# State space: half of the gate product computed ahead during the scan chain, and three of eight final multiplications on GpSimd

## The chip, the cores and the metric

The kernel runs on one core of one Trainium2 chip. The time is the device time of one execution in microseconds (us). PE is TensorE, DVE is VectorE, ACT is ScalarE, POOL is GpSimd, and SP is SyncE, which here only issues transfers.

## What is computed

The program is one layer of a decoder trunk over 2048 positions: norm, input projection, attention, spatial gating and state space, output projection, feed-forward, and a gated embedding. The change lies in the state space (all fp32, 256 channels, 16 groups of 16 with 64 complex states each):

```
y = Re(C x) + D u                         # x: scan over the positions
y = gelu(y)                               # [2048, 256]
y = y * sigmoid(y @ glu_w + glu_b)        # the gate product, K = 256
```

## The kernel before

`state_space` (L1220) is one stage of its own; a barrier ends it. Positions are held as 256 chunks of 8 (`L`), the 256 chunks as two halves of 128 (`HM`), so that the output tile `Y` is [128, 2, 8, 256]. The 16 groups are worked off in 8 pairs (`Q`), called group 0 to 7 below.

DVE (L1511 to L1526) does two pairs at a time: it turns, scans along the chunks, and turns back into `entry`; a memset of `mark` (L1526) tells PE that two pairs are ready. PE (L1384 to L1399) then makes for each pair and chunk half a product with the entry states, two with the Toeplitz kernels and one more with the entry states (L1394, L1396, L1398) into bank q. ACT (L1440 to L1446) takes each bank through the gelu into `Y`.

The gate product needs `Y` with channels on the partitions. `turn_y(k)` (L1360) transposes channel half k in 16 tiles into banks 4k to 4k+3, and ACT copies these into `yT` (L1439 and L1449), which lies over the input `U`. Half 0 is turned ahead of pair 6 (`q == Q - 2`), half 1 behind pair 7. Also ahead of pair 6 stands `gate_product()` (L1376, work for the next stage's row tile 0, in bank 4), which DVE finishes in `finish_gate` and follows with `combine`. When all eight copies are there, PE runs the gate product (L1405 to L1410): 16 tiles of 128 positions, two channel halves each, two tiles to a bank:

```python
for n in range(HM * L):
    for k in range(2):
        mm = pe.matmul(bank[n // 2][...], yT[:, k, n * P:(n + 1) * P], glu_w[:, k, :], start=(k == 0), stop=(k == 1))
```

For each bank DVE adds the bias, which is spread over the partitions (`add_glu_bias`, L1529), ACT takes the sigmoid (L1453), and DVE multiplies `Y` by it (`apply_gate`, L1535), two banks behind the addition (L1540 to L1544). SP stores `Y` in four pieces (L1289 to L1292), each when its four positions of the chunk are done, and then loads row tile 0 for the next stage (L1294), `mix_and_project`, whose first ACT operation (L1718) waits for it.

POOL in this stage clears tiles, copies weights, adds the diagonal, masks four tiles (L1314) and does three steps of the normalisation of row tile 0 (L1318 to L1322); it has nothing after that. All queues are written out by hand; there is no planner. `Ba` and `Ca` of `StateParameters` (L702) are read by PE's first transposes and kernel products and by POOL's weight copies, and are idle later. The matmuls that the prediction compares with are those of L1345 (spreading of u, 64 output partitions) and L1182 (a lookup in the projection stage, over 33 partitions); the operations on POOL and DVE that it compares with are of the feed-forward (L2918, L2931, L2955; L2632, L2651) and of the projection (L1209).

Of the kernel before, what the change touches and what calls it, by code (L numbers as in the profile page):

```python
# [22 lines left out]
P = 128  # L23
# [647 lines left out]
CH = 16  # L671
# [26 lines left out]
class StateParameters:  # L698
# [4 lines left out]
    def __init__(self, nc, keep, p, ident, M):  # L703
        self.nc, self.p, self.ident = nc, p, ident
        self.Q, self.M = p["a_re"].shape[0] // 2, M
        Q, at = self.Q, SSM_AT
        self.turn_table = keep.over("turn", [P, 2, Q, M], F32, at)
        self.Ba = keep.over("Ba", [P, 2, Q, L, CH], F32, at + 2 * Q * M * 4)
        self.Ca = keep.over("Ca", [P, 2, Q, L + 1, CH], F32, at + 2 * Q * (M + L * CH) * 4)
        self.radius = keep.over("radius", [P, Q], F32, at + 2 * Q * (M + (2 * L + 1) * CH) * 4)  # L710
        assert at + (2 * Q * (M + (2 * L + 1) * CH) + Q) * 4 == SBUF_END
# [508 lines left out]
def state_space(nc, U, u_loaded, p, parameters, mix, ident, loads_ahead, part_stored, part_stores, mix_ahead, mix_ahead_loads):  # L1220
# [17 lines left out]
    MASK_AT, MASK_BANK, GATE_BANK = 2, Q - 1, 4  # L1238
    with Stage(nc, "ssm") as st:
# [22 lines left out]
            st.sem(n) for n in ("y_turned", "yT_copied", "entry_ready", "y_ready", "gelu_ready", "glu_done", "sig_ready", "out_ready"))  # L1262
        b_turned, b_copied, k_done, k_copied, share_done, share_copied = (
# [8 lines left out]
        @block.sync  # L1272
        def _(sp):
            z0, z0_src, z0_loaded = mix_ahead_loads[0]
            sp.dma_start(z0, z0_src).then_inc(z0_loaded, DMA)
            sp.dma_start(d_cols[:, :], p["d"].rearrange("(g c) -> c g", c=CH), allow_slow_non_contiguous=True).then_inc(d_loaded, DMA)
            sp.dma_start(glu_w[:, :, :], p["glu_w"].rearrange("(k p) n -> p k n", p=P)).then_inc(glu_loaded, DMA)
            sp.dma_start(glu_b[:, :], p["glu_b"].unsqueeze(0).to_broadcast([P, W])).then_inc(glu_loaded, DMA)
            for stored_part, count in zip(part_stored, part_stores):
                sp.wait_ge(stored_part, count)  # L1280
            for tile, src, loaded in mix_ahead_loads[1:]:
                sp.dma_start(tile, src, allow_slow_non_contiguous=True).then_inc(loaded, DMA)
            sp.wait_ge(kernel_ready, 1)
            sp.wait_ge(cleared, 1)
            for j in range(L):
                sp.dma_start(toeplitz[j * CH:(j + 1) * CH, :, j * CH:], kernel_rows[:, :, 0:(L - j) * CH]).then_inc(toeplitz_copied, DMA)
            for part, src, loaded in loads_ahead:
                sp.dma_start(part, src).then_inc(loaded, DMA)
            for h in range(HM):  # L1289
                for l in range(0, L, 4):  # L1290
                    sp.wait_ge(out_ready, h * L + l + 4)
                    sp.dma_start(mix_view[:, h, l:l + 4], Y[:, h, l:l + 4]).then_inc(stored[h], DMA)  # L1292
            sp.wait_ge(stored[0], L // 4 * DMA)
            sp.dma_start(ahead.row0[:, heads * HEAD + GW:], mix[0:P, :]).then_inc(ahead.row0_loaded, DMA)  # L1294

        @block.gpsimd
        def _(pool):
# [13 lines left out]
            pool.wait_ge(weights_ready, 4)  # L1311
            pool.wait_ge(mix_ahead.setup, 5 * DMA)
# [9 lines left out]
            nc.gpsimd.tensor_tensor(ahead.normed0[:, :, :], d, ahead.ln_shift.rearrange("p (g c) -> p g c", g=GROUPS), ALU.add).then_inc(ahead.normed_ready, 1)  # L1322

        @block.tensor
        def _(pe):
# [57 lines left out]

            for q in range(Q):  # L1384
                if q == MASK_AT:
                    turn_masks()
                if q == Q - 2:
                    turn_y(0)
                    gate_product()
                pe.wait_ge(entry_ready, q // 2 + 1)  # L1390
# [12 lines left out]
            pe.wait_ge(glu_loaded, 2 * DMA)  # L1403
            pe.wait_ge(yT_copied, 8)
            for n in range(HM * L):  # L1405
                for k in range(2):
                    mm = pe.matmul(bank[n // 2][:, (n % 2) * W:(n % 2 + 1) * W], yT[:, k, n * P:(n + 1) * P], glu_w[:, k, :],
                                   start=(k == 0), stop=(k == 1))
                if n % 2:
                    mm.then_inc(glu_done, 1)  # L1410

        @block.scalar
        def _(act):
# [17 lines left out]
            nc.scalar.activation(ahead.weight[:, :, :], ahead.drop[:, :, :], ACT.Exp, scale=-1.0).then_inc(ahead.weight_ready, 1)  # L1431
            for q in range(Q):
# [3 lines left out]
                if q == Q - 2:  # L1436
                    for n in range(4):
                        act.wait_ge(y_turned, n + 1)
                        nc.scalar.copy(yT.rearrange("p k t -> p (k t)")[:, n * BANK:(n + 1) * BANK], bank[n][:, :]).then_inc(yT_copied, 1)  # L1439
                act.wait_ge(y_ready, q + 1)  # L1440
# [15 lines left out]
        def _(dve):  # L1456
# [72 lines left out]
            def add_glu_bias(n):  # L1529
                h, l = divmod(2 * n, L)  # L1530
                dve.wait_ge(glu_done, n + 1)
                V.tensor_tensor(gate[:, h, l:l + 2, :], bank[n].rearrange("p (l w) -> p l w", l=2),
                                glu_b[:, :].unsqueeze(1).to_broadcast([P, 2, W]), ALU.add).then_inc(sig_ready, 1)

            def apply_gate(n):  # L1535
                h, l = divmod(2 * n, L)
                dve.wait_ge(rooted, 1 + n)
                V.tensor_tensor(Y[:, h, l:l + 2, :], Y[:, h, l:l + 2, :], gate[:, h, l:l + 2, :], ALU.mult).then_inc(out_ready, 2)

            for n in range(HM * L // 2 + 2):  # L1540
                if n < HM * L // 2:
                    add_glu_bias(n)
                if n >= 2:
# [1802 lines left out]
```

## Time and profile before

| | us |
|---|---|
| median of 3 runs | 2675.37 |
| lowest, highest | 2674.75, 2676.18 |
| the profiled execution's own time | 2676.85 |
| its span in the profile | 2675.3 |
| busy: PE, PE weight loads | 2532.1, 2169.0 |
| busy: DVE, ACT, POOL | 1794.4, 1352.9, 828.5 |

The profile is of one execution. The span runs from the first to the last recorded instruction; what lies around it is in the own time only. Busy times overlap between engines. An fp32 matmul leaves two records, a transpose one, so the gate product's 32 products are 64 records. In a list in order of time, instructions of one line that follow each other are merged; the second number is then the time that all of them took. The granted clock of PE is given as a share of 2.4 GHz.

### The profile page before, as it was taken

Reading aid. Unit: us, or ns where it says so; the run is one execution under the profiler, and the core shown is the slowest. Engines: PE = TensorE matmul, PEld = TensorE weight load, DVE = VectorE, ACT = ScalarE, POOL = GpSimd, SP = SyncE. Lnnn points to the kernel's source line nnn. Section 1 sums busy time; section 2 is a strip of 40 time slices with the busy share of each in tenths; the row PEclk is TensorE's granted clock in tenths of the full one; section 3 lists DMA queues with packets and bytes.
Section 4 is the critical chain, followed back from the end, with each engine's and each line's share of the span. In section 5 each row is a group of like instructions: output and inputs, shape, how many; then the busy total and the mean of one; then the engine's idle time right before and its main releaser. Section 6 shows DMA issues by size and latency. Waiting matters only on the chain. (4 is left out here: it accounts for less than half of the span.)

```text
span 2675.3 us, 38121 instructions
## 1 busy us (share of the span) xinstructions
PE 2532.1 (95%) x13395; PEld 2169.0 (81%) x13395; DVE 1794.4 (67%) x3337; ACT 1352.9 (51%) x2431; POOL 828.5 (31%) x625
## 2 busy tenths in 40 slices
PE   7999999999976899699999989999999999999998
PEld 6989979999965788488888868888888877887876
DVE  1113287777775776699999966879889975563333
ACT  4343424666645666455555546545555553444444
POOL 4454554655521111246555530002122210000000
PEclk9999999999987899799999999999999999999999
DMA  6675466788653454244444577543333336763221
GB/s 219 187 217 177 160 185 166 175 182 182 143 139 127 136 174 171 65 136 155 157 154 162 176 257 263 194 144 100 101 103 111 103 126 228 283 222 114 79 73 48
DMA packets 317450, 420.97 MB, mean 157 GB/s; under 512 B 31073, under 2 KB 229025, under 8 KB 312522
## 3 DMA queue, kind: packets, MB, share of 16 engines
q1 hardware_dynamic: 292090, 332.68, 41.4%
q0 software_dynamic: 25184, 86.01, 8.6%
q8 instruction: 102, 1.67, 0.3%
q14 instruction: 74, 0.61, 0.1%
HBM read 298.59 MB, written 124.16 MB: 158 GB/s over the span
## 5 line engine op out<-in xcount | busy, mean ns | idle before, releaser
L2834 PE MATMUL ffn_bank<-ffn_x,ffn_ring 128*128 128x512 f32 x704 | 278.1, 395 | 17.2 <-DVE ffn_strips L2632 8.9
L2836 PE MATMUL ffn_bank<-ffn_x,ffn_ring 128*128 128x512 f32 x704 | 277.2, 394 | 0.0
L2835 PE MATMUL ffn_bank<-ffn_x,ffn_ring 128*128 128x512 f32 x704 | 277.2, 394 | 0.0
L2908 POOL DMA_DIRECT2D ffn_act<-ffn_late x154 | 85.7, 558 | 476.1 <-DVE ffn_late L2664 445.4
L1203 POOL TENSOR_TENSOR in_w_lo<-in_w,in_w_hi 128x2048 fp32r<-128x2048 f32 x36 | 168.1, 4670 | 173.5 <-ACT in_w_hi L1071 173.5
L2834 PE MATMUL ffn_bank<-tail_shared,ffn_ring 128*128 128x512 f32 x528 | 206.3, 391 | 9.1 <-DVE ffn_ring L2607 7.5
L633 ACT ACTIVATE att_exps<-att_scores,att_part 128x256 f32<-128x256 f32 (+1 forms) x384 | 153.0, 454 | 105.1 <-DVE att_part L601 104.3
L2836 PE MATMUL ffn_bank<-tail_shared,ffn_ring 128*128 128x512 f32 x528 | 205.9, 390 | 0.0
L2431 ACT COPY ffn_strips<-ffn_bank 128x512 f32<-128x512 f32 x176 | 103.5, 588 | 147.6 <-PE ffn_bank L2836 147.6
L2648 DVE SCALAR_TENSOR_TENSOR ffn_strips<-ffn_strips,ffn_taps 128x512 f32<-128x512 f32 x176 | 144.6, 822 | 43.4 <-ACT ffn_strips L2446 43.4
L2834 PEld LDWEIGHTS ffn_bank<-ffn_x,ffn_ring 128*128 128x128 f32 x704 | 134.0, 190 | 49.0 <-issue 13.1
L2836 PEld LDWEIGHTS ffn_bank<-ffn_x,ffn_ring 128*128 128x128 f32 x704 | 134.1, 190 | 28.3
L2615 DVE TENSOR_TENSOR ffn_ring<-ffn_w,ffn_ring 128x2048 fp32r<-128x2048 f32 (+1 forms) x42 | 91.0, 2167 | 98.0 <-ACT ffn_ring L2405 98.0
L571 PE MATMUL att_bank<-att_v,att_expsT 128*128 128x66 f32 x1200 | 153.7, 270 | 2.8 <-issue 2.4
L2835 PEld LDWEIGHTS ffn_bank<-ffn_x,ffn_ring 128*128 128x128 f32 x704 | 134.0, 190 | 27.6
L571 PEld LDWEIGHTS att_bank<-att_v,att_expsT 128*128 128x128 f32 x1200 | 147.3, 192 | 4.5 <-issue 2.8
L1175 PE MATMUL in_bank<-in_w_hi,in_hi 128*128 128x256 f32 x512 | 145.8, 285 | 0.0
L2651 DVE SCALAR_TENSOR_TENSOR ffn_strips<-ffn_strips,ffn_taps 128x512 f32<-128x512 f32 x176 | 141.5, 804 | 6.2
L1176 PE MATMUL in_bank<-in_w_lo,in_hi 128*128 128x256 f32 x512 | 144.8, 283 | 0.0
L1177 PE MATMUL in_bank<-in_w_hi,in_lo 128*128 128x256 f32 x512 | 144.8, 283 | 0.0
L2396 ACT CAST ffn_ring<-ffn_sums 128x512 fp32r<-128x512 f32 x176 | 107.9, 614 | 62.5 <-PE ffn_bank L2836 52.0
L2835 PE MATMUL ffn_bank<-ffn_x_lo,ffn_ring 128*128 128x512 f32 x352 | 136.9, 389 | 0.0
(441 smaller groups left out, 7369.3 us busy)
## 6 DMA issues: line engine op xcount, KB each, us to landing
ffn_w<-in_ffn_w_up SPq DMA_DIRECT2D x88, 512.0 KB, 4.8
ffn_act<-ffn_late POOLq DMA_DIRECT2D x154, 256.0 KB, 2.3
in_w<-in_w_in SPq DMA_DIRECT2D x36, 1024.0 KB, 6.6
ffn_a_raw<-ffn_act SPq DMA_DIRECT2D x77, 256.0 KB, 3.5
ffn_a_raw_later<-ffn_act SPq DMA_DIRECT2D x77, 256.0 KB, 4.4
ffn_w<-ffn_down_sums SPq DMA_DIRECT2D x16, 1024.0 KB, 5.1
ffn_w<-in_ffn_w_down SPq DMA_DIRECT2D x12, 1024.0 KB, 5.8
ffn_pieces<-in_ffn_w_down POOLq DMA_DIRECT2D x44, 256.0 KB, 3.6
```

The costliest lines, as they stand in the source:

```text
L571: mm = pe.matmul(out, expsT[:, n % 2, piece * P:(piece + 1) * P], vals[:, b, blk, h * ROW:(h + 1) * ROW], start=(at == 0), stop=(at == len ...
L633: nc.scalar.activation(exps[:, n % RING, m * width:(m + 1) * width], scores[:, n % RING, m * width:(m + 1) * width], ACT.Exp, bias=part[:, ...
L1175: pe.matmul(out[:, 0:WIDE], x_hi[:, k, part], w_hi[w][:, k, :], start=(k == 0), stop=False)
L1176: pe.matmul(out[:, 0:WIDE], x_hi[:, k, part], w_lo[w][:, k, :], start=False, stop=False)
L1177: mm = pe.matmul(out[:, 0:WIDE], x_lo[:, k, part], w_hi[w][:, k, :], start=False, stop=(k == KC - 1))
L1203: nc.gpsimd.tensor_tensor(w_lo[B % 2][:, :, :], w_raw[B % 2][:, :, :], w_hi[B % 2][:, :, :].bitcast(F32), ALU.subtract).then_inc(w_lo_read ...
L2396: nc.scalar.copy(slot(j)[0], src).then_inc(w_hi_ready, 1)
L2648: nc.vector.scalar_tensor_tensor(conv[:, n, tg], raw[f % 2][:, n, 1 + tg * BANK:1 + (tg + 1) * BANK], tap[1], conv[:, n, tg], ALU.mult, AL ...
L2651: nc.vector.scalar_tensor_tensor(conv[:, n, tg], raw[f % 2][:, n, tg * BANK:(tg + 1) * BANK], tap[0], conv[:, n, tg], ALU.mult, ALU.add).t ...
L2834: pe.matmul(out[:, :], hi[:, k], x_hi[kind][:, k], start=(k == 0 and fresh), stop=False, skip_group_check=not fresh)
L2835: pe.matmul(out[:, :], hi[:, k], x_lo[kind][:, k], start=False, stop=False, skip_group_check=not fresh)
L2836: mm = pe.matmul(out[:, :], lo[:, k], x_hi[kind][:, k], start=False, stop=(k == KH - 1), skip_group_check=not fresh)
```

## The change

The first channel half of the gate product is computed during the scan chain. The turn of half 0 moves from pair 6 up to pair 4. There PE makes, for banks 0 to 3 (position tiles 0 to 7), a product of a row of ones with the bias (one partition, 256 columns) and on top of it that of channel half 0; ACT copies each bank to the new tile `glu_sums`. Ahead of pair 6, behind `gate_product()`, the same is done for tiles 8 to 15 in the same four banks. At the end PE makes only the products of channel half 1, and each group of four tiles waits for its own copy of `yT` (from the ninth tile on, for all). DVE adds the kept sum instead of the bias. `glu_sums` and the ones lie over `Ba` and `Ca`. POOL multiplies banks 1, 3 and 5 by their gates instead of DVE, and SP waits for both counts.

```diff
     def __init__(self, nc, keep, p, ident, M):        # StateParameters
+        glu_at, glu_end = at + 2 * Q * M * 4, at + 2 * Q * (M + (2 * L + 1) * CH) * 4
+        self.glu_first = keep.over("glu_first", [P, M * L // P, 2 * P], F32, glu_at)
+        self.ones = keep.over("glu_ones", [P, P], F32, glu_at + M * L * 2 * 4)
...
+    EARLY_AT, LATE_AT, EARLY_BANKS = Q // 2, Q - 2, 4
+    POOL_GATES = (1, 3, 5)
...
                 for l in range(0, L, 4):
-                    sp.wait_ge(out_ready, h * L + l + 4)
+                    s = (h * L + l) // 4
+                    sp.wait_ge(out_ready, 2 * s + 2 - sum(n < 2 * s + 2 for n in POOL_GATES))
+                    sp.wait_ge(pool_out_ready, sum(n < 2 * s + 2 for n in POOL_GATES))
...
             pool.wait_ge(weights_ready, 4)
+            nc.gpsimd.memset(ones[0:1, :], 1.0).then_inc(ones_ready, 1)
...
+            for n in POOL_GATES:
+                h, l = divmod(2 * n, L)
+                pool.wait_ge(rooted, n + 1)
+                nc.gpsimd.tensor_tensor(Y[:, h, l:l + 2, :], Y[:, h, l:l + 2, :], gate[:, h, l:l + 2, :], ALU.mult).then_inc(pool_out_ready, 1)
...
+            def first_glu_products(first):
+                for b in range(first, first + EARLY_BANKS):
+                    for i in range(2):
+                        n = 2 * b + i
+                        out = bank[b % EARLY_BANKS][:, i * W:(i + 1) * W]
+                        pe.matmul(out, ones[0:1, :], glu_b[0:1, :], start=True, stop=False)
+                        mm = pe.matmul(out, yT[:, 0, n * P:(n + 1) * P], glu_w[:, 0, :], start=False, stop=True)
+                    mm.then_inc(early_done, 1)
+
             for q in range(Q):
...
-                if q == Q - 2:
+                if q == EARLY_AT:
                     turn_y(0)
+                    pe.wait_ge(glu_loaded, 2 * DMA)
+                    pe.wait_ge(ones_ready, 1)
+                    pe.wait_ge(yT_copied, 4)
+                    first_glu_products(0)
+                if q == LATE_AT:
                     gate_product()
+                    pe.wait_ge(early_kept, EARLY_BANKS)
+                    first_glu_products(EARLY_BANKS)
...
             turn_y(1)
-            pe.wait_ge(glu_loaded, 2 * DMA)
-            pe.wait_ge(yT_copied, 8)
+            pe.wait_ge(early_kept, 2 * EARLY_BANKS)
             for n in range(HM * L):
-                for k in range(2):
-                    mm = pe.matmul(bank[n // 2][:, (n % 2) * W:(n % 2 + 1) * W], yT[:, k, n * P:(n + 1) * P], glu_w[:, k, :],
-                                   start=(k == 0), stop=(k == 1))
+                if n % 4 == 0:
+                    pe.wait_ge(yT_copied, 4 + n // 4 + 1 if n < 2 * EARLY_BANKS else 8)
+                mm = pe.matmul(bank[n // 2][:, (n % 2) * W:(n % 2 + 1) * W], yT[:, 1, n * P:(n + 1) * P], glu_w[:, 1, :], start=True, stop=True)
...
+            def keep_first_glu(first):
+                for b in range(first, first + EARLY_BANKS):
+                    act.wait_ge(early_done, b + 1)
+                    nc.scalar.copy(glu_sums[:, 2 * b:2 * b + 2, :], bank[b % EARLY_BANKS].rearrange("p (l w) -> p l w", l=2)).then_inc(early_kept, 1)
...
-                if q == Q - 2:
+                if q == EARLY_AT:
                     for n in range(4):
                         act.wait_ge(y_turned, n + 1)
                         nc.scalar.copy(yT...)
+                    act.wait_ge(weights_ready, 4)
+                    keep_first_glu(0)
+                if q == LATE_AT:
+                    keep_first_glu(EARLY_BANKS)
...
             def add_glu_bias(n):
+                dve.wait_ge(early_kept, n + 1)
                 dve.wait_ge(glu_done, n + 1)
                 V.tensor_tensor(gate[:, h, l:l + 2, :], bank[n].rearrange("p (l w) -> p l w", l=2),
-                                glu_b[:, :].unsqueeze(1).to_broadcast([P, 2, W]), ALU.add).then_inc(sig_ready, 1)
+                                glu_sums[:, 2 * n:2 * n + 2, :], ALU.add).then_inc(sig_ready, 1)
...
-                if n >= 2:
+                if n >= 2 and n - 2 not in POOL_GATES:
                     apply_gate(n - 2)
```

## Rows read from the trace of the kernel before

**Rows 1.** The waits between 744 and 842 us: total us, times, longest.

```profile
DVE ssm_share L1532 <- PE ssm_bank L1407: 10.7, 8, 6.5
...
PE ssm_bank L1394 <- DVE ssm_mark L1526: 7.6, 2, 6.0
```

**Rows 2.** DVE in order of time: start, us, line, operation, [idle before <- releaser].

```profile
803.49 0.06 DVE L1526 MEMSET ssm_mark<- 128x1 f32 x1
...
827.03 0.69 DVE L1532 TENSOR_TENSOR ssm_share<-ssm_bank,ssm_glu_b 128x512 f32<-128x512 f32 x1 [0.44 <-PE ssm_bank L1407]
827.64 1.89 DVE L1538 TENSOR_TENSOR ssm_Y<-ssm_Y,ssm_share 128x512 f32<-128x512 f32 x3
```

**Rows 3.** PE in order of time, the same columns.

```profile
782.11 0.70 PE L1394 MATMUL ssm_bank<-ssm_Ca_pair,ssm_spun 128*128 128x256 f32 x2 [1.62 <-DVE ssm_mark L1526]
...
787.02 0.60 PE L1398 MATMUL ssm_bank<-ssm_Ca_pair,ssm_spun 128*128 128x256 f32 x2
793.57 1.22 PE L1394 MATMUL ssm_bank<-ssm_Ca_pair,ssm_spun 128*128 128x256 f32 x2 [5.96 <-DVE ssm_mark L1526]
...
800.77 1.91 PE L1365 MATMUL ssm_bank<-whole_ident,ssm_Y 128*128 128x128 f32 x16
802.51 1.00 PE L1381 MATMUL ssm_bank<-ixers_ahead_normed,mixers_ahead_maskT 128*128 128x64 f32 x8
803.61 0.70 PE L1394 MATMUL ssm_bank<-ssm_Ca_pair,ssm_spun 128*128 128x256 f32 x2
...
810.08 1.94 PE L1365 MATMUL ssm_bank<-whole_ident,ssm_Y 128*128 128x128 f32 x16 [0.97 <-ACT ssm_Y L1444]
812.94 14.05 PE L1407 MATMUL ssm_bank<-ssm_glu_w,whole_u 128*128 128x256 f32 x64 [0.93 <-ACT whole_u L1449]
```

**Rows 4.** ACT in order of time, the same columns.

```profile
787.65 0.79 ACT L1444 ACTIVATE ssm_Y<-ssm_bank 128x128 f32<-128x128 f32 x4 [1.83 <-PE ssm_bank L1398]
...
809.15 0.79 ACT L1444 ACTIVATE ssm_Y<-ssm_bank 128x128 f32<-128x128 f32 x4 [1.83 <-PE ssm_bank L1398]
810.75 2.06 ACT L1449 COPY whole_u<-ssm_bank 128x512 f32<-128x512 f32 x4 [0.81 <-PE ssm_bank L1365]
812.82 1.28 ACT L1453 ACT_TABLE_LOAD   x1
```

**Rows 5.** SP's issue of row tile 0 and ACT's wait for it.

```profile
829.93 0.46 SPq L1294 DMA_DIRECT2D mixers_ahead_row<-ssm_out  x1
...
835.04 0.63 ACT L1718 ACTIVATE mixed_squares<-mixers_ahead_row 128x512 f32<-128x512 f32 x1 [6.65 <-DMA mixers_ahead_row<-ssm_out]
```

**Rows 6.** Two other products: the spreading of u, and the lookup of the bias.

```profile
762.16 3.67 PE L1345 MATMUL ssm_bank<-whole_u,ssm_BaT 128*64 128x256 f32 x32 [0.23 <-ACT ssm_kernel_rows L1422]
...
L1182 PE MATMUL in_bank<-in_lookup,in_per_head x6: 804/844/844, 12.2 to 15.3; 33*8 33x384 f32 x6
```

**Rows 7.** POOL's and DVE's operations of 512 columns beside each other.

```profile
L2918 POOL TENSOR_TENSOR ffn_late<-ffn_late x22: 1286/1296/1847, 1153.4 to 2190.3; 128x512 f32<-128x512 f32 x22
...
L1209 POOL TENSOR_TENSOR in_result_lo<-in_result,in_result_hi x32: 1268/1300/2408, 41.2 to 402.0; 128x512 fp32r<-128x512 f32 x32
...
1479.07 1.07 POOL L2955 TENSOR_TENSOR ffn_pieces<-ffn_pieces 128x256 f32<-128x256 f32 x1
...
1487.43 1.56 POOL L2931 TENSOR_TENSOR ffn_late<-ffn_late 128x512 f32<-128x512 f32 x1
...
1479.46 0.68 DVE L2632 TENSOR_TENSOR ffn_strips<-ffn_bank,ffn_strips 128x512 f32<-128x512 f32 x1
...
1487.87 1.67 DVE L2651 SCALAR_TENSOR_TENSOR ffn_strips<-ffn_strips,ffn_taps 128x512 f32<-128x512 f32 x1
...
1490.84 0.75 DVE L2651 SCALAR_TENSOR_TENSOR ffn_strips<-ffn_strips,ffn_taps 128x512 f32<-128x512 f32 x1
```

**Rows 8.** Granted clock (PEclk) in short stretches, with each engine's busy time.

```profile
782.00:787.60 5.60, 5.49 (x32) 4.75 (x32) 5.53 (x7) 0.79 (x4) 4.14 (x3) 1.00 0.20 82
...
791.00:793.40 2.40, 0.00 (x0) 0.00 (x0) 2.36 (x3) 0.00 (x0) 0.00 (x0) 0.50 0.00 0
```

More of the change, by code:

```diff
@@ L710, in __init__ @@
         self.radius = keep.over("radius", [P, Q], F32, at + 2 * Q * (M + (2 * L + 1) * CH) * 4)
+        glu_at, glu_end = at + 2 * Q * M * 4, at + 2 * Q * (M + (2 * L + 1) * CH) * 4
+        self.glu_first = keep.over("glu_first", [P, M * L // P, 2 * P], F32, glu_at)
+        self.ones = keep.over("glu_ones", [P, P], F32, glu_at + M * L * 2 * 4)
+        assert glu_at + (M * L * 2 + P) * 4 <= glu_end
         assert at + (2 * Q * (M + (2 * L + 1) * CH) + Q) * 4 == SBUF_END
@@ L1262, in state_space @@
             st.sem(n) for n in ("y_turned", "yT_copied", "entry_ready", "y_ready", "gelu_ready", "glu_done", "sig_ready", "out_ready"))
+        glu_sums, ones = parameters.glu_first, parameters.ones
+        ones_ready, early_done, early_kept, pool_out_ready = (st.sem(n) for n in ("ones_ready", "early_done", "early_kept", "pool_out_ready"))
         b_turned, b_copied, k_done, k_copied, share_done, share_copied = (
@@ L1537, in apply_gate @@
                 dve.wait_ge(rooted, 1 + n)
-                V.tensor_tensor(Y[:, h, l:l + 2, :], Y[:, h, l:l + 2, :], gate[:, h, l:l + 2, :], ALU.mult).then_inc(out_ready, 2)
+                V.tensor_tensor(Y[:, h, l:l + 2, :], Y[:, h, l:l + 2, :], gate[:, h, l:l + 2, :], ALU.mult).then_inc(out_ready, 1)
             for n in range(HM * L // 2 + 2):
```

## The prediction, made before the changed kernel was run

> **What bounds the kernel now.** The change lies in one stage, the state space, some 80 us of a span of 2675.3. I read the waits of that stage first, then each engine's instructions in order of time. The waits [rows 1] show that the engines hand over to each other: in the middle PE waits 7.6 us for DVE's mark, which closes a pair of groups, and at the end DVE waits 10.7 us for the gate product, 6.5 of it for the first bank.
>
> So the stage has two parts. Up to 803.5 DVE sets the pace: it has no gaps between its scan chains, and the last mark stands at 803.49 [rows 2]. PE idles in that part: groups 2 and 3 end at 787.0 + 0.6 = 787.6, groups 4 and 5 start at 793.57 when their mark comes [rows 3]. After 803.5 it is PE. Groups 6 and 7, their gelu and the start of the second turn take 803.61 to 810.08, that is 6.47; the gate product starts at 812.94, 2.86 behind the turn, because it waits for all four of ACT's copies; its 64 records run to 827.0 [rows 3, 4]. DVE only follows: its last bias addition starts at 827.03, 0.04 behind PE, then sigmoid, and three multiplications, the last of which ends at 827.64 + 1.89 = 829.53 [rows 2]. SP then issues the load of row tile 0 (829.93), and the next stage opens on it: ACT's first square starts at 835.04, 5.1 behind the issue, after 6.65 of waiting [rows 5]. What is won or lost at 829.53 is therefore won or lost in the kernel.
>
> **The change, part by part.** The price of a matmul first. The fp32 product of 256 columns leaves two records; 64 records from 812.94 to 812.94 + 14.05 are 0.2195 each, 0.439 a product [rows 3].
> - *Gone from the end*: the first channel half, 16 products, 16 x 0.439 = 7.02 us.
> - *Added earlier*: the same 16 products, 7.02, and 16 products of the ones row with the bias, 256 columns each. I take 0.439 for these too, another 7.02. No row has a product over one partition. The lower end is the pair of 64-wide outputs over 256 columns, 32 records in 3.67, 0.115 each [rows 6]: half price, 3.7 us in all. The nearest by partitions is the lookup product over 33: five steps between 12.2 and 15.3, 0.62 for 384 columns, 1.61 ns a column against 0.86 in the gate product [rows 6]. That would be 13.2 us. It is nearly twice the gate product's pace, as the lower of the clock's two levels would make it, so I read it as clock and not as a price of few partitions; it does say that few partitions are not cheap.
>
> *Where the added work lies.* The turn of the first half moves from 800.77 up to group 4. It needs the gelu of group 3, which ends at 787.65 + 0.79 = 788.44 [rows 4]; with the 0.14 that lay between gelu and turn before (809.94 to 810.08) it starts at 788.58. Copies and first product follow 2.86 later, 791.44, as at the end of before. The first batch (8 bias, 8 halves) is 7.02: PE is free at 798.46. Groups 4 and 5 were ready at 793.46, and now wait 5 us for PE. They take 5.4, as groups 2 and 3 did (782.11 to 787.6 [rows 3]): 803.9. The gate statistics' product 1.1 (802.51 to 803.61): 805.0. The second batch 7.02: 812.0. Groups 6 and 7 with gelu 6.47: the second turn starts at 818.5, not at 810.08. PE's idle 6 us and the low-clock stretch in groups 4 and 5 are used up, and **PE becomes the bound from 788 to the end**; 8.4 us later is what the 14 us of early work cost beyond the cover.
>
> *What comes back.* The first product no longer waits for all copies, only for one of the second half: 16 transposes end 16 x 0.11 = 1.8 after the turn's start (1.91 for 16 before), the first copy is done by then (0.67 + 0.6). So 818.5 + 1.8 = 820.3, a gain of 1.1; the 16 remaining products end at 827.3. The last addition starts 0.04 after, about 827.4, against 827.03. The eight additions read a kept sum in place of the bias; partitions and columns are the same, so 0.69 each.
>
> *Copies of the kept sums*, 8 x 0.6 on ACT [rows 4]: four lie in ACT's idle time before group 4's gelu; PE waits for the first four before the second batch, but they end near 799. The second four end about 0.6 behind the batch, before group 6's gelu is due. ACT's table load for the sigmoid (1.28 behind the last copy) ends near 822.5; the first addition ends at 822.1, so the first sigmoid is 0.4 late, and catches up at 0.63 against 0.88 a bank. Nothing at the end. SP has one more wait, POOL one memset of one partition that only the masks follow, the four semaphores no row: no time.
>
> *The three multiplications on POOL.* DVE had 0.61 a multiplication (1.89 for three). PE now gives a bank every 0.88, not 1.75, and DVE's 16 operations at 0.61 to 0.65 would take 10 us for banks that come in 7: without the move the end would be near 831. With it DVE has 13. POOL's 512-column operation takes 1.29 alone [rows 7], but the two engines stop each other. With both operands in the state buffer, DVE's 0.75 became 1.67 from 1487.87, under POOL's operation from 1487.43 to 1488.99, whereas an addition with one operand in PSUM kept its 0.68 under POOL [rows 7]. So the additions go free, the multiplications take turns. In order: multiplication 0 on DVE until 824.4; POOL's 1 until 825.7; DVE's 2 until 826.3; POOL's 3 until 827.6; DVE's 4 until 828.2; the last addition behind it until 828.9, its sigmoid until 829.6; POOL's 5 until 829.5; DVE's 6 until 830.1 and 7 until 830.7. Against 829.53: **+1.2**. Bounds: nothing in each other's way gives 827.4 + 0.69 + 0.04 + 0.63 + 0.04 + 0.68 = 829.5, no loss; POOL at 2.4 each, the longest of its 32 operations of this size [rows 7], three in a row from 823.7, gives 830.9 and two multiplications, 832.1, +2.6.
>
> The Trainium skill (SBUF — State Buffer, "Who interferes with whom") calls this an exclusive lock between a GpSimd instruction that reads SBUF and a VectorE instruction with two SBUF inputs. By that rule the end is +1.2, without it +0; these rows agree with it.
>
> **The sum.** -7.0 (products) + 8.4 (second turn late) - 1.1 (first product earlier) = +0.3, tail +0.9 on top: +1.2. The profiled execution took 2676.85 (span 2675.3 and 1.55 around it), 1.48 above the median of 2675.37; the sum makes it 2678.05, and the median **2676.6**. Nothing behind the stage is changed, and its opening load follows the end of the multiplications as before. About 0.2% (5.35 us) is what a measurement of this kernel can tell from no change: faster begins below 2670.0, slower above 2680.7.
>
> **The rivals.**
> - *A, the forecast*: PE, not DVE, bounds the middle, and the gain at the end is paid for ahead of it. 0.72.
> - *B, the bias products cost little.* At half price the second turn comes 3.5 earlier: -2.3, 2673.1, still no change. At no price it would start at 811.4, bound by the mark at 803.49 + 0.1 and what follows: with a tail like A's 830.7 - 7.0 = 823.7, -5.8, 2669.6, faster. For: the spreading products (L1345) at half. Against: they write 64 partitions at a time, first one half of the bank's rows and then the other; here all 128 are written. 0.05 for half, 0.04 for none.
> - *C, slower: the clock.* In before PE's granted clock fell from 1.00 to 0.50 (2.4 to 1.2 GHz) after it had idled from 787.6; 791.0 to 793.4 is at 0.50 [rows 8]; group 4's first products, behind it, took 1.22 where those of group 2 took 0.70 [rows 3], which DVE hid. Now PE has only 16 short transposes in the 3.8 us between 787.6 and 791.44, and what runs then is on the path. Half of all time at 0.50 is lost: a spell of 6 us from 791 costs 3, giving 2679.6: no change still. It decides from (5.35 - 1.2) x 2 = 8.3 us at 0.50: the whole first batch, 14 us at that level, costs 7.0 and gives 2683.6. For: the row at 791.0; against: 782.0 to 787.6 was at 1.00 behind a pause of 1.6 [rows 3, 8]. 0.12 for the short spell, 0.04 for the long one.
> - *D, the early part does not get early* (a mark or a copy comes so late that the batches queue behind it): the marks do not depend on PE, so this only gives what A has. 0.03, up to 2681.5.
>
> The Trainium skill (TensorE: Matmul & The Clock Gate, "Part 4: PE-mode transpose") says that a transpose doesn't count as PE work for the clock as other matmuls do. By this rule C's short spell would happen and the time be 2679.6. No row before decides: the transposes at 800.77 ran at 1.00 behind other products.
>
> **How the numbers follow.** A with its bounds (-1.2 for no conflict on DVE, +1.4 for POOL at its slowest) reaches from 2675.4 to 2678.0; C's short spell lies at 2679.6 and B at half price at 2673.1. Range 2673.0 to 2680.3: it takes these in with 0.7 for the terms' errors on the upper side, and leaves out C long, B at no price and most of D. Faster: B at no price, and 0.01 for errors at A's lower end, 0.05. Slower: C long, and 0.02 for half of D and the 33-partition price, 0.06. Same: 0.89.
>
> **What would show it.** Right: matmul records of the batches from about 791.4 to 798.5 and 805 to 812 without a gap, bias ones at 0.22; group 4's products start near 798.5, 5 behind their mark; second turn near 818.5; 32 records of the final product in 7.0; POOL's multiplications near 1.3, and DVE's beside them over 1; last multiplication near 830.7. Wrong: a second turn before 815 (bias products cheap), granted clock at 0.50 between 791 and 812 (C), a last multiplication at 829.5 or 832 (tail mis-sized), or a difference that arises behind 835, which none of this covers.

## The result, and the profile after

The changed kernel takes 2697.54 us (median of 4, 2695.03 to 2700.12) against 2675.77 for the kernel before (median of 4, the three of the table above and one more): a ratio of 1.0081, interval 1.0067 to 1.0094. It is slower by some 21 us, where +1.2 and no measurable change were forecast. The profiled execution took 2698.17, with a span of 2696.6: 21.3 us more than the 2675.3 of before.

Where the 21.3 lie can be read from four points. The stage begins with PE's first transposes. In the profile of before:

```profile
748.93 3.03 PE L1330 MATMUL ssm_bank<-whole_ident,whole_Ba 128*128 128x128 f32 x16 [2.65 <-PEq L143]
```

PE of the changed kernel in order of time (start, us, line, operation and count, [idle before <- releaser]); it answers to [rows 3]:

```profile
751.85 3.47 PE L1345 MATMUL ssm_bank<-whole_ident,whole_Ba 128*128 128x128 f32 x16 [2.65 <-PEq L143]
...
791.08 1.97 PE L1380 MATMUL ssm_bank<-whole_ident,ssm_Y 128*128 128x128 f32 x16 [0.88 <-ACT ssm_Y L1483]
793.97 0.67 PE L1404 MATMUL ssm_bank<-ssm_glu_b,whole_glu_ones 1*128 1x256 f32 x2 [0.92 <-ACT whole_u L1474]
794.57 0.70 PE L1405 MATMUL ssm_bank<-ssm_glu_w,whole_u 128*128 128x256 f32 x2
...
796.45 1.22 PE L1404 MATMUL ssm_bank<-ssm_glu_b,whole_glu_ones 1*128 1x256 f32 x2
797.60 1.22 PE L1405 MATMUL ssm_bank<-ssm_glu_w,whole_u 128*128 128x256 f32 x2
...
810.11 1.06 PE L1425 MATMUL ssm_bank<-ssm_Ca_pair,ssm_spun 128*128 128x256 f32 x2
...
817.02 1.00 PE L1396 MATMUL ssm_bank<-ixers_ahead_normed,mixers_ahead_maskT 128*128 128x64 f32 x8
817.95 0.69 PE L1404 MATMUL ssm_bank<-ssm_glu_b,whole_glu_ones 1*128 1x256 f32 x2
...
824.62 1.22 PE L1404 MATMUL ssm_bank<-ssm_glu_b,whole_glu_ones 1*128 1x256 f32 x2
...
831.39 1.06 PE L1425 MATMUL ssm_bank<-ssm_Ca_pair,ssm_spun 128*128 128x256 f32 x2
...
839.03 1.94 PE L1380 MATMUL ssm_bank<-whole_ident,ssm_Y 128*128 128x128 f32 x16 [0.97 <-ACT ssm_Y L1483]
840.81 7.07 PE L1438 MATMUL ssm_bank<-ssm_glu_w,whole_u 128*128 128x256 f32 x32
```

DVE of the changed kernel, the same columns; it answers to [rows 2]:

```profile
806.08 0.06 DVE L1565 MEMSET ssm_mark<- 128x1 f32 x1
...
841.94 0.69 DVE L1572 TENSOR_TENSOR ssm_share<-ssm_bank,whole_glu_first 128x512 f32<-128x512 f32 x1 [18.97 <-PE ssm_bank L1438]
...
849.07 1.76 DVE L1578 TENSOR_TENSOR ssm_Y<-ssm_Y,ssm_share 128x512 f32<-128x512 f32 x2
```

and ACT's first square of the next stage, which answers to [rows 5]:

```profile
856.00 0.63 ACT L1758 ACTIVATE mixed_squares<-mixers_ahead_row 128x512 f32<-128x512 f32 x1 [6.18 <-DMA mixers_ahead_row<-ssm_out]
```

The stage starts 2.9 later (751.85 against 748.93), before any edited line runs. Its last multiplication ends at 849.07 + 1.76 = 850.83 against 829.53. So the stage, from first transpose to last multiplication, is 98.98 us against 80.60, **+18.4**. The first square follows 5.2 behind (5.5 before), and from there to the end it is 1840.6 against 1840.3. All that the change did is in the stage. The 2.9 ahead of it is scatter: in a second profile of the kernel before (before_again, below) the stage starts at 751.60.

Inside the stage the last mark stands 54.2 behind the first transpose, as before (54.6): DVE's chain is untouched. What is late is PE's second turn, at 839.03, 33.0 behind the last mark; before it was 6.6, and the forecast had 15.0 (818.5 - 803.49). From the second turn to the end it is 11.8 against 19.45; forecast 12.2. The gain at the end came as foreseen, 7.65. The price ahead of it was 26.4, not 8.4.

Read the batches in PE's rows. A pair of records of the bias product and a pair of the half alternate. From 793.97 they follow each other at 0.60 to 0.63 us a pair, from 796.45 at 1.15; the forecast had 0.439. PE's weight loads (PEld) show where the first part of that comes from, in the gate product of before and then in the changed kernel:

```profile
812.91 13.68 PEld L1407 LDWEIGHTS ssm_bank<-ssm_glu_w,whole_u 128*128 128x128 f32 x64 [1.13 <-issue]
```

```profile
794.57 0.30 PEld L1405 LDWEIGHTS ssm_bank<-ssm_glu_w,whole_u 128*128 128x128 f32 x2 [0.33 <-issue]
795.20 0.29 PEld L1404 LDWEIGHTS ssm_bank<-ssm_glu_b,whole_glu_ones 1*128 1x128 f32 x2 [0.33 <-issue]
```

In before the 64 loads, 0.19 each, keep the pace of the matmuls above them (13.68 us in all). In the changed kernel no load runs for 0.33 ahead of each pair, and a pair's loads start only when the pair before is nearly done (794.57, the time at which PE's row of that pair begins too).

For the second part, the clock says what the doubling from 0.6 to 1.15 is (stretch, length, busy us and instructions of PE, its loads, DVE, ACT, POOL, then the granted clock, DMA share and GB/s):

```profile
793.97:796.45 2.48, 2.48 (x8) 1.15 (x9) 2.40 (x5) 0.00 (x0) 0.00 (x0) 1.00 0.00 0
796.45:810.10 13.65, 13.65 (x25) 6.34 (x25) 9.42 (x14) 1.75 (x3) 0.00 (x0) 0.50 0.00 0
...
817.95:824.40 6.45, 6.45 (x21) 3.04 (x20) 4.67 (x9) 1.23 (x3) 0.00 (x0) 0.95 0.00 0
824.60:831.40 6.80, 6.80 (x14) 3.34 (x14) 0.00 (x0) 0.58 (x1) 0.00 (x0) 0.50 0.00 0
```

Two things came together. At a granted clock of 1.00 a pair takes 0.625 and not 0.439; and from 796.4 and again from 823.8 the clock is at 0.50 (1.2 in place of 2.4 GHz), although PE was busy all of that time (13.65 of 13.65 us in the first stretch).

### The profile page after: what moved, and what is told of

Its sections match the earlier page's. It is cut to its first block and busy times, and to the rows that moved or that the text cites. A ratio compares the mean times of both kernels' runs of the same rounds, so it can differ in the third digit from the quotient of the medians.

```text
span 2696.6 us, 38199 instructions
## 1 busy us (share of the span) xinstructions
PE 2551.5 (95%) x13427; PEld 2175.8 (81%) x13427; DVE 1793.8 (67%) x3334; ACT 1357.6 (50%) x2439; POOL 831.9 (31%) x629
## 3 DMA queue, kind: packets, MB, share of 16 engines
q8 instruction: 102, 1.67, 0.3%
## 5 line engine op out<-in xcount | busy, mean ns | idle before, releaser
L2875 PEld LDWEIGHTS ffn_bank<-ffn_x,ffn_ring 128*128 128x128 f32 x704 | 133.3, 189 | 27.3
```

Of the source, the lines that this page charges most:

```text
L2875: pe.matmul(out[:, :], hi[:, k], x_lo[kind][:, k], start=False, stop=False, skip_group_check=not fresh)
```

## The experiments

The stage's length is compared from the profiles, since it is free of the scatter before and behind. T is the second turn's distance from the last mark, E the distance from the second turn to the end of the last multiplication. Each ratio is to runs of the kernel before made beside that variant (their medians are 2675.8, 2675.9, 2676.4 and 2678.5), so it isn't the quotient of two medians of this column.

| kernel | first transpose | last multiplication's end | stage | T | E | median us | ratio to before (interval) |
|---|---|---|---|---|---|---|---|
| before | 748.93 | 829.53 | 80.60 | 6.6 | 19.45 | 2675.77 | |
| before_again | 751.60 | 831.87 | 80.27 | 6.6 | 19.4 | 2677.02 (one run) | |
| after | 751.85 | 850.83 | 98.98 | 33.0 | 11.8 | 2697.54 | 1.0081 (1.0067 to 1.0094) |
| after_again | 751.43 | 844.89 | 93.46 | 26.7 | 11.8 | 2689.82 (one run) | |
| no_bias | 754.39 | 829.46 | 75.07 | 9.0 | 11.8 | 2674.24 | 0.9985 (0.9970 to 1.0000) |
| rows128 | 751.54 | 833.53 | 81.99 | 16.0 | 11.8 | 2678.47 | 1.0003 (0.9987 to 1.0018) |
| rows64 | 751.81 | 838.16 | 86.35 | 20.3 | 11.8 | 2687.19 | 1.0036 (1.0022 to 1.0050) |
| rows32 | 751.42 | 845.79 | 94.37 | 28.3 | 11.8 | 2695.25 (one run) | |
| ones_first | 751.38 | 838.91 | 87.53 | 21.5 | 11.8 | 2684.98 | 1.0026 (1.0013 to 1.0039) |
| bias_dve | 750.77 | 824.50 | 73.73 | 7.4 | 11.8 | 2674.63 | 0.9992 (0.9983 to 1.0001) |
| bias_dve_again | 750.88 | 825.97 | 75.09 | 9.0 | 11.8 | 2674.32 | 0.9990 (0.9980 to 1.0000) |
| bias_dve_dve_gates | 753.39 | 828.15 | 74.76 | 7.4 | 13.1 | 2673.10 | 0.9992 (0.9983 to 1.0001) |
| pool_gates_only | 752.63 | 833.70 | 81.07 | 7.0 | 19.0 | 2679.57 | 1.0012 (1.0003 to 1.0021) |

One more thing varies between the profiles and has to be kept apart. In six of the thirteen, PE's clock is at 0.50 for some 3 us in groups 2 and 3, ahead of every batch, although all their products are over 128 partitions: before_again, no_bias, rows128, rows32, ones_first and bias_dve_again. The kernel before itself does it in one profile and not in the other:

```profile
786.00:788.00 2.00, 2.00 (x8) 1.72 (x8) 1.97 (x2) 0.00 (x0) 1.84 (x3) 0.50 0.01 4
```

(before_again, the same columns as above; the first profile has 1.00 there.) DVE hides it in before. In the changed program the first turn follows group 3, so there it costs 1.67 us: from the start of group 2 to the first turn it is 6.38 in after and 8.05 in rows128.

The theory (P): the bias product stands on one partition, between products over 128. The weights of a product of another height are not loaded ahead, and a PE on which one partition works in half of the products is given the lower clock. The rivals: any batch put early costs this (E), or the number of products does (W).

**no_bias**: the bias products taken out (and the bias with them).

```diff
-                        pe.matmul(out, ones[0:1, :], glu_b[0:1, :], start=True, stop=False)
-                        mm = pe.matmul(out, yT[:, 0, ...], glu_w[:, 0, :], start=False, stop=True)
+                        mm = pe.matmul(out, yT[:, 0, ...], glu_w[:, 0, :], start=True, stop=True)
```

> The changed kernel without the 16 bias products (the bias is left out of the result). Theory P (the product over one partition, between products over 128, makes each weight load wait for the matmul ahead of it, 0.3125 us a record in place of 0.2195, and PE so thinly filled falls to the lower clock): without them a batch of 8 halves takes 8 x 0.439 = 3.5 us, the granted clock stays 1.00 from 791 on, the second turn comes about 8 us behind the last mark as in before, and the time is 2670 or a little under. Rival E (any early batch ahead of a group does it: little work behind 16 transposes drops the clock, whatever the products are over): the halves run at 0.58 a record, the batches take 7 each, and the time is 2680 or more.

PE of this run, in order of time:

```profile
798.19 3.69 PE L1404 MATMUL ssm_bank<-ssm_glu_w,whole_u 128*128 128x256 f32 x16 [0.92 <-ACT whole_u L1473]
...
807.79 3.67 PE L1404 MATMUL ssm_bank<-ssm_glu_w,whole_u 128*128 128x256 f32 x16
...
817.67 1.94 PE L1380 MATMUL ssm_bank<-whole_ident,ssm_Y 128*128 128x128 f32 x16 [0.97 <-ACT ssm_Y L1482]
```

Each batch is 3.7, the pace of before, and the stage is 5.5 shorter than before. E falls: an early batch behind 16 transposes costs its products and no more. The whole was 2674.24, where 2670 was expected, 0.9985 of before, with an interval that ends at 1.0000: the stage shows the gain, the whole time barely. T is 9.0, where bias_dve below, with the same program on PE, has 7.4: this is the 1.67 of groups 2 and 3 at the lower clock.

**rows128**: the same product, spread over all partitions.

```diff
-            nc.gpsimd.memset(ones[0:1, :], 1.0)
+            nc.gpsimd.memset(ones[0:128, :], 1.0 / 128)
...
-                        pe.matmul(out, ones[0:1, :], glu_b[0:1, :], start=True, stop=False)
+                        pe.matmul(out, ones[0:128, :], glu_b[0:128, :], start=True, stop=False)
```

> The bias product over 128 partitions, each row of ones being 1/128: the same number of products and columns, the same result. Theory P: no change of height between products, batches of 7.0 us, clock 1.00, second turn at about 12 us behind the last mark, time 2676 to 2678, what the prediction said. Rival W (it is the number of products and the accumulation on a just started bank that cost, not the one partition): batches of 13 to 16 us as in the changed kernel, time 2697.

```profile
795.85 0.59 PE L1405 MATMUL ssm_bank<-ssm_glu_w,whole_u 128*128 128x256 f32 x2
796.28 0.59 PE L1404 MATMUL ssm_bank<-ssm_glu_b,whole_glu_ones 128*128 128x256 f32 x2
...
801.89 0.59 PE L1405 MATMUL ssm_bank<-ssm_glu_w,whole_u 128*128 128x256 f32 x2
...
821.73 1.94 PE L1380 MATMUL ssm_bank<-whole_ident,ssm_Y 128*128 128x128 f32 x16 [0.97 <-ACT ssm_Y L1483]
```

A pair each 0.43, the batch 7.0, as the prediction priced it; the stage 82.0, **+1.4 where the prediction said +1.2**, the ratio 1.0003. That the two agree so closely is luck: 1.67 of rows128's stage is the lower clock in groups 2 and 3. Without it the stage would be near 80.3 and T 14.3, so the forecast sum was about 1.5 too high (T 0.7, the tail 0.4, the marks 0.3). The 12 for T in the expectation of this run was too low. The number of products, the weight loads and the accumulation are those of the changed kernel; only the partitions differ. W falls, and the 17 us between 99.0 and 82.0 (11.5 with the second profile of the changed kernel) hang on the height of sixteen products.

**ones_first**: in each batch the eight bias products first, then the eight halves.

```diff
...
+                for n, out in tiles:
+                    pe.matmul(out, ones[0:1, :], glu_b[0:1, :], start=(n % 2 == 0), stop=False, skip_group_check=True)
+                for n, out in tiles:
+                    mm = pe.matmul(out, yT[:, 0, ...], glu_w[:, 0, :], start=False, stop=(n % 2 == 1), skip_group_check=True)
...
```

> The eight bias products of a batch in a row, then its eight halves: the same instructions, two changes of height a batch in place of sixteen. If the slow pace comes from each change of height (P1), records are at 0.22 again and a batch takes 7.0 to 7.5 us at full clock; the clock then says whether one-partition products count less for it: if not, time 2677; if they do, it falls during or behind the eight, and the time lies at 2680 to 2690. If the slow pace belongs to every one-partition product wherever it stands (P2), the eight take 0.31 a record or more, and the halves 0.22.

PE in order of time, and then stretches with the granted clock:

```profile
795.19 3.69 PE L1402 MATMUL ssm_bank<-ssm_glu_b,whole_glu_ones 1*128 1x256 f32 x16 [0.92 <-ACT whole_u L1474]
798.80 5.41 PE L1404 MATMUL ssm_bank<-ssm_glu_w,whole_u 128*128 128x256 f32 x16
804.05 0.59 PE L1425 MATMUL ssm_bank<-ssm_Ca_pair,ssm_spun 128*128 128x256 f32 x2
...
810.22 4.96 PE L1402 MATMUL ssm_bank<-ssm_glu_b,whole_glu_ones 1*128 1x256 f32 x16
```

```profile
795.19:798.90 3.71, 3.71 (x17) 2.95 (x17) 3.63 (x6) 0.00 (x0) 0.00 (x0) 1.00 0.00 0
799.00:802.00 3.00, 3.00 (x8) 2.38 (x9) 2.86 (x7) 0.59 (x1) 0.00 (x0) 0.50 0.00 0
...
814.00:818.00 4.00, 4.00 (x10) 2.71 (x10) 1.20 (x2) 0.59 (x1) 0.00 (x0) 0.50 0.00 0
```

Sixteen one-partition records run in 3.69, 0.22 each: a product over one partition is no dearer and no cheaper than one over 128, and in the first batch no slow pace is left. That is P1: the slow pace belongs to the change of height. But the clock still falls: in the first batch it is 1.00 in the eight bias products and 0.50 from 799 on, while halves over 128 partitions run; in the second it falls already within the eight, which take 4.96. The slow pace is gone and the fall is not, so the fall isn't caused by exposed loads. The time, 2685, is at the middle of the third outcome expected.

**rows64** and **rows32**: as rows128, with 64 partitions and 1/64, or 32 and 1/32.

> The bias product over 64 partitions with 1/64. If only products over the whole height let the next weight load go ahead (P1 with any smaller height), the pace stays 0.31 and the clock decides the rest: if it follows the pace, 2697; if it follows the number of rows at work, which is now near three quarters, it stays at 1.00 and the time is 2682 to 2684 (6 us of exposed loads over the forecast). If the pace is 0.22, the price is of one partition alone.

PE over 64 partitions, and the clock in both batches:

```profile
793.95 0.67 PE L1404 MATMUL ssm_bank<-ssm_glu_b,whole_glu_ones 64*128 64x256 f32 x2 [0.92 <-ACT whole_u L1474]
794.55 0.70 PE L1405 MATMUL ssm_bank<-ssm_glu_w,whole_u 128*128 128x256 f32 x2
795.18 0.70 PE L1404 MATMUL ssm_bank<-ssm_glu_b,whole_glu_ones 64*128 64x256 f32 x2
...
803.87 0.59 PE L1425 MATMUL ssm_bank<-ssm_Ca_pair,ssm_spun 128*128 128x256 f32 x2
```

```profile
793.95:803.87 9.92, 9.92 (x32) 4.92 (x33) 9.67 (x15) 1.75 (x3) 0.00 (x0) 1.00 0.00 0
810.04:819.99 9.95, 9.95 (x34) 4.93 (x33) 4.67 (x9) 1.81 (x4) 0.00 (x0) 1.00 0.00 0
```

In this profile the two terms come apart. The pairs follow each other at 0.628 as over one partition, and the clock stays at 1.00 in both batches and beside them. So a product of half height costs the same exposed load as one of one partition, and here it cost no clock. The batch, 9.9, is 2.9 above rows128's 7.0, for 16 changes of height: 0.18 each, about as long as one weight load of the gate product in before (0.190 on average). So what is paid at each change is about one weight load that is no longer hidden. The two batches make 6.0 us; the stage is only 4.4 above that of rows128 because rows128 had the 1.67 in groups 2 and 3. The whole time missed the expected 2682 to 2684: the median of ten runs is 2687.19 (2682.30 to 2691.09), and the profiled one, 2682.91, is the second fastest. Whether the clock fell in the slower ones isn't known, since only one was profiled.

> The bias product over 32 partitions with 1/32. The pace stays at 0.31 as over 64 and over 1 (height changes). If the clock follows the share of rows at work, it lies between one partition (falls) and 64 (stays at 1.00): with 32 of 128 in half of the products it may go either way; stays: stage 86 to 88 us; falls: 95 to 99.

```profile
795.24:805.00 9.76, 9.76 (x32) 4.76 (x33) 9.51 (x15) 1.76 (x3) 0.00 (x0) 1.00 0.00 0
816.50:826.00 9.50, 9.50 (x18) 4.54 (x18) 0.00 (x0) 1.17 (x2) 0.00 (x0) 0.50 0.00 0
```

The stage is 94.4, in the range expected if the clock falls. With 32 partitions the clock held in the first batch and was at 0.50 in the second: between the two, as far as two batches can tell.

**bias_dve**: no bias products; DVE adds the bias to the kept sums in the time in which it waits for PE.

```diff
...
             combine()
+            dve.wait_ge(glu_loaded, 2 * DMA)
+            for n in range(HM * L // 2):
+                dve.wait_ge(early_kept, n + 1)
+                kept = glu_sums[:, 2 * n:2 * n + 2, :]
+                V.tensor_tensor(kept, kept, glu_b[:, :].unsqueeze(1).to_broadcast([P, 2, W]), ALU.add).then_inc(bias_added, 1)
...
-                dve.wait_ge(early_kept, n + 1)
+                dve.wait_ge(bias_added, n + 1)
```

> The changed kernel without bias products; DVE adds the bias to the eight kept sums behind its work for row tile 0, where it waited 19 us before the last bank-by-bank additions. Theory: 8 additions at 0.61 to 0.69 fit between about 5 us behind the last mark and the end of the second turn (9 behind the mark in the run without bias), so the stage is as long as in that run, 75.1 us from the first transpose to the last multiplication against 80.6 before: 5.5 us less, 2670.4. Rival: the additions end behind the first bank of the final product and delay the tail by up to 2 us: 77, 2672.

DVE in order of time, and PE's second turn:

```profile
805.32 0.06 DVE L1562 MEMSET ssm_mark<- 128x1 f32 x1
...
810.20 4.90 DVE L1569 TENSOR_TENSOR whole_glu_first<-whole_glu_first,ssm_glu_b 128x512 f32<-128x512 f32 x8
815.60 0.69 DVE L1575 TENSOR_TENSOR ssm_share<-ssm_bank,whole_glu_first 128x512 f32<-128x512 f32 x1 [0.51 <-PE ssm_bank L1435]
...
822.74 1.76 DVE L1581 TENSOR_TENSOR ssm_Y<-ssm_Y,ssm_share 128x512 f32<-128x512 f32 x2
```

```profile
812.69 1.94 PE L1379 MATMUL ssm_bank<-whole_ident,ssm_Y 128*128 128x128 f32 x16 [0.97 <-ACT ssm_Y L1480]
```

The eight additions end at 815.10 and the first of the final ones starts at 815.60, still waiting for PE: they cost nothing. The stage is 73.7, **6.9 shorter than before and 20 to 25 shorter than the changed kernel**, at the full result. The 75.1 expected was no_bias's, with the lower clock in groups 2 and 3; this profile doesn't have it. T is 7.4 against 6.6, so PE is nearly back on DVE's mark.

In the whole this is worth less than it should be: the median is 2674.63 and not 2670.4, the ratio 0.9992. Repeated:

> The version with the bias on DVE again, since its first ratio (0.9992, interval 0.9983 to 1.0001) is smaller than its stage's gain (6.9 of 80.6 us, 0.9974). If the stage's gain holds in the whole, the stage is 73.7 again and the two ratios together lie under 1; if something behind the stage takes it back, the time from the first square to the end is above that of the kernel before by more than the runs scatter.

0.9990 (0.9980 to 1.0000), with a stage of 75.1 and not 73.7: the lower clock was back in groups 2 and 3. Both intervals just reach 1. Averaged as two independent measurements they give about 0.9991 with 0.0007 to each side (an estimate), which lies under 1 and is some 2.4 us, against 5 to 7 in the stage. From the first square to the end these two profiles have 1843.8 and 1842.5 us (for bias_dve, 2673.6 - 829.79), those of before 1840.3 and 1838.4, but other variants have 1836.7 to 1842.4. Whether something behind the stage takes back 3 us, or only scatter does, stays open.

**The POOL part.** bias_dve_dve_gates is bias_dve with `POOL_GATES = ()`; pool_gates_only is the kernel before with the three multiplications on POOL.

> The same, with all eight final multiplications on DVE. The prediction's term: DVE's 16 operations at 0.61 to 0.65 come later than PE's banks, and the end lies near 10 us behind the first addition, against the 8.9 measured with three on POOL: second turn to end 12.5 to 13.0 in place of 11.8, the time 1 us above the one with POOL. Rival (POOL's operations cost DVE as much as they save): 11.8 again.

> The kernel before with only the three multiplications on POOL. PE gives a bank each 1.75 us there and DVE has room, so nothing is won: the end is set by the last addition, its sigmoid and multiplication 7; multiplication 5 on POOL frees one of the three that DVE does at the end, 0 to 0.6 us less; second turn to end 18.9 to 19.5 against 19.45, the time unchanged.

The last multiplications of the first (three on DVE), and of the second on POOL and DVE:

```profile
826.26 1.89 DVE L1581 TENSOR_TENSOR ssm_Y<-ssm_Y,ssm_share 128x512 f32<-128x512 f32 x3
```

```profile
829.60 1.27 POOL L1330 TENSOR_TENSOR ssm_Y<-ssm_Y,ssm_share 128x512 f32<-128x512 f32 x1 [2.18 <-ACT ssm_share L1461]
```

```profile
830.50 0.92 DVE L1546 TENSOR_TENSOR ssm_Y<-ssm_Y,ssm_share 128x512 f32<-128x512 f32 x1
...
832.23 1.47 DVE L1546 TENSOR_TENSOR ssm_Y<-ssm_Y,ssm_share 128x512 f32<-128x512 f32 x2
```

With PE giving a bank each 0.88, the move to POOL is worth 13.14 - 11.81 = 1.3 us in the tail: DVE is the bound of the tail without it. The whole time doesn't show it: without the move it is 2673.10 against 2674.63, both at a ratio of 0.9992, where 1 us more was expected. With a bank each 1.75 it is worth 0.4 (19.45 to 19.03), and DVE's multiplication at 830.50, which begins under POOL's (829.60 to 830.87), takes 0.92 in place of 0.68. The whole of that kernel was 1.0012 (1.0003 to 1.0021), though the stage explains only 0.5 us of 3.

**Second profiles.**

> The kernel before once more, for a second profile. If the stage's length is a property of the kernel, it is again 80.6 us within 0.5 from the first transpose to the last multiplication; what lies ahead of the stage (748.9 in the first profile, 750.8 to 754.4 in the others) and behind it (1836.7 to 1843.8 from the first square to the end) moves from run to run by several us without the change.

> The changed kernel once more: batches at 0.31 a record at the higher clock, and again falls of the clock in both; stage 99 us, within 3, since the point in a batch at which the clock falls may move.

The stage of before is 80.3 again. That of the changed kernel is 93.5 in place of 99.0, outside the 3 us expected. The clock now fell at 801.7 and 822.2, not at 796.4 and 823.8, and came back sooner, so that 14 us in place of 27 were at 0.50. The exposed loads (6 us) are the same in both. The lower clock cost some 12 us in the first profile and 6 in the second, where T is 6.3 shorter.

## Why the prediction was wrong, by its own steps

**The price of the bias product** is the step that failed: "I take 0.439 for these too". The product itself does take 0.44 (ones_first: 16 records in 3.69 us). What was left out is what it does to its neighbours: each change of height exposes a weight load (6.0 us in all), and the clock falls (12.2 us). The first alone would have made the forecast 2682.6 in place of 2676.6, above the stated range. In the profiled execution the late second turn is made of:

| | us |
|---|---|
| forecast distance from the last mark | 15.0 |
| height changes: 32 x 0.186 (a pair at 0.625 against 0.439) | 6.0 |
| batch 1 at 0.50: 16.1 measured against 10.0 at that pace | 6.1 |
| batch 2 at 0.50: 13.4 against 10.0 | 3.4 |
| groups 4 and 5 behind it: 6.9 against 5.4 | 1.5 |
| groups 6 and 7 to the turn: 7.6 against 6.5 | 1.2 |
| sum | 33.2, measured 33.0 |

The batches are 810.11 - 793.97 and 831.39 - 817.95; 10.0 is 32 records at 0.3125. The last 0.2 is the gate statistics' product, 0.93 where 1.1 was taken.

**The row that could not show it**: the lookup over 33 partitions at 1.61 ns a column. It was read as clock, and that fits: the transposes right behind it are 13 in the 2.62 us from 16.48 to 19.10 and 21 in the 2.20 from 19.20, 0.20 and 0.10 each, so the first of them ran at half pace. (The column of the granted clock reads 1.00 for both stretches, but the trace's first entry for the clock is only at 19.14.) All products of the lookup are over 33 partitions, so it says nothing of a change of height. The spreading products, at the other end, showed small outputs cheap. In before, products of different heights meet only here and there (at 756.3, 760.0 and 1096.1, for instance) and never alternate. The bounds were taken for the product alone and not for the sequence.

**The clock (rival C)**: the mechanism was named with its price, but as a consequence of PE's pause and the transposes, with 0.16 in all, and its long form put at 2683.6. Behind pause and transposes the clock did not fall (no_bias, rows128: 1.00 from 792 on, in both batches and the groups). It fell behind one-partition products, and once behind products over 32. The argument against C, that 782.0 to 787.6 was at 1.00 behind a pause of 1.6, was a single profile's: before_again has 0.50 there, behind a pause of 2.2. Its price, 1.67, is not in the sum, though it didn't fall due in the profiled execution of the changed kernel. The rule drawn from the Trainium skill (TensorE: Matmul & The Clock Gate, Part 4: PE-mode transpose) would have made a short spell here: these traces do not show one. C's cost of half of all time at 0.50 holds: 12.2 us of it are in the table, for 27.3 us at 0.50 (stretches of 2 us put it at 796.4 to 813.5 and 823.8 to 834.0), a little under half, since a pair took 1.15 there and not twice 0.625.

**Rival B** (cheap bias products) was wrong: 0.22 a record in ones_first.

**That PE becomes the bound of the middle** was right: in rows128, which is the change as it was priced, PE has no gap from the first batch to group 7, and T is 16.0 against 15.0 forecast, 14.3 without the lower clock in groups 2 and 3.

**The tail** was right in size and reason: 11.8 against 12.2. POOL's multiplications in the changed kernel:

```profile
844.29 1.80 POOL L1337 TENSOR_TENSOR ssm_Y<-ssm_Y,ssm_share 128x512 f32<-128x512 f32 x1 [55.18 <-ACT ssm_share L1492]
846.30 1.59 POOL L1337 TENSOR_TENSOR ssm_Y<-ssm_Y,ssm_share 128x512 f32<-128x512 f32 x1 [0.21 <-ACT ssm_share L1492]
```

1.80 and 1.59 where 1.29 was taken for one alone, since the turns with DVE's are in them; the additions kept 0.69 beside them. bias_dve_dve_gates gives the other side, 13.1.

**The comparison with the median** was right: the ends of the span, and what lies behind the stage, did not change.

## What to carry to other kernels

A price per instruction holds for a sequence only if the sequence is like the one that it was read from: before putting a small matmul between full ones, look for rows in which both stand side by side, and if there are none, widen the range for the neighbours and not only for the instruction. A bias or another rank-one term belongs on an engine that waits anyway (here DVE, 4.9 us at no cost), or, if it must be on PE, over the full height (rows of 1/128), or at least all such products in a row, which saved the exposed loads but not the clock (stage 87.5 against 82.0). Work moved under a chain of another engine is free only up to that engine's slack: here 6 us of PE's idle time against 14 of work.

## What the runs showed of the hardware

A matmul over 1, 32 or 64 partitions between matmuls over 128 exposes about one weight load at each change of height, 0.19 us at the higher clock (pairs at 0.625 to 0.628 against 0.43 to 0.44), and nothing between matmuls of the same height, be it 1 or 128 (0.22 a record in ones_first and in before). That is for fp32 products of 256 columns. The Trainium skill (TensorE: Matmul & The Clock Gate, Part 3, "The mechanism") says that LDWEIGHTS overlaps with matmuls in flight only when the row group differs, though its first paragraph also lets a load into the background weight buffer go ahead. Of the rule with "only", these traces show the opposite: loads over the same 128 partitions hid entirely, 64 records at 0.2195 with loads of 0.19, and those that changed the height did not.

PE's granted clock fell to 0.50 within batches in which PE was busy without a gap: in four of four in which products over one partition alternate with products over 128 (after, after_again), in both of ones_first, in one of two over 32, and in none of the two over 64, the two of rows128 and the eight without bias products. Outside the batches it fell in full-height work too, in groups 2 and 3 of six profiles, about 1 us after PE had come back from a pause of 1.95 to 2.3 (after had one of 1.96 and no fall). Busy time on PE's row does not show this; the clock's column does. Why fewer partitions bring the clock down is open.
